# The copy of the transposed inverse in the block inverse: from VectorE to ScalarE

## The reference, cut to what matters

```
state = state * w_t + (state @ a_t) b_t + v_t k_t
y_t   = state @ r_t
```

## Time and profile before

| | |
|---|---|
| Three timed runs | 870.73, 872.73, 873.32 us; median 872.73 |
| Profiled execution | 871.72 us, its span (first to last instruction) 869.7 us |
| Granted TensorE clock | 0.997 of full speed |
| Busy share of the span | PE 99%, DVE 77%, ACT 56%, POOL 14% |

### The profile page before, as it was taken

How to read it: one execution, slowest core, us unless ns; L and a number is a source line. 1 busy time by engine, 2 the same in 40 slices (tenths; PEclk the granted TensorE clock), 3 DMA queues, 4 the chain that set the end, 5 groups by cost and what they waited for, 6 DMA issues and landing times.

```text
span 869.7 us, 19047 instructions
## 1 busy us (share of the span) xinstructions
PE 858.3 (99%) x7516; PEld 780.2 (90%) x7516; DVE 671.0 (77%) x999; ACT 486.8 (56%) x783; POOL 119.0 (14%) x136
## 2 busy tenths in 40 slices
PE   7999999999999999999999999999999999999998
PEld 7998988888888998898888888899999988899997
DVE  6996988877767776768877777787897686758876
ACT  5675465555544656745555554448824346456574
POOL 2002400000122000031000006660003500100010
PEclk9999999999999999999999999999999999999999
DMA  9543555554456542245555545576433443434461
GB/s 333 193 151 115 177 188 193 193 193 148 167 198 219 187 146 98 97 147 194 190 182 182 182 154 179 187 263 210 144 126 122 124 123 124 105 128 155 157 222 49
DMA packets 23410, 144.50 MB, mean 166 GB/s; under 512 B 2968, under 2 KB 3224, under 8 KB 9648
## 3 DMA queue, kind: packets, MB, share of 16 engines
q1 hardware_dynamic: 22032, 140.26, 47.0%
q0 software_dynamic: 1168, 3.23, 1.9%
q10 hardware_dynamic: 144, 0.06, 0.0%
HBM read 142.47 MB, written 1.06 MB: 165 GB/s over the span
## 4 chain that ended last, share of the span: by engine, by line
PE 87%; DVE 9%; ACT 1%; issue 1%; DMA 1%; SPq 0%; DVEq 0%; ACTq 0%
PE ps L615 28%; PE ps L612 14%; PE ps L602 10%; PE ps L603 10%; PE ps L604 10%; PE ps L1055 7%; DVE lo L2183 2%; DVE X L2198 1%; DMA MEM<-in_mem 1%; PE ps L758 1%; PE ps L909 1%; DVE lo L2621 1%; PE ps L759 1%; PE ps L760 1%; DVE PR L2767 1%
## 5 line engine op out<-in xcount | busy, mean ns | idle before, releaser
L615 PE MATMUL ps<-X,hi 128*128 128x512 f32 x800 | 254.7, 395 | 0.0
L2183 DVE TENSOR_TENSOR lo<-raw,hi 128x1024 fp32r<-128x1024 f32 (+1 forms) x210 | 244.1, 1204 | 10.3 <-ACT hi L1564 7.1
L612 PEld LDWEIGHTS ps<-X,lo 128*128 128x128 f32 x800 | 150.1, 188 | 32.4 <-issue 1.3
L612 PE MATMUL ps<-X,lo 128*128 128x256 f32 x800 | 165.9, 279 | 0.5 <-DVE lo L2183 0.4
L602 PE MATMUL ps<-X,hi 128*128 128x256 f32 x504 | 146.3, 290 | 0.0
L603 PE MATMUL ps<-X,hi 128*128 128x256 f32 x504 | 142.5, 283 | 0.0
L604 PE MATMUL ps<-X,lo 128*128 128x256 f32 x504 | 142.5, 283 | 0.0
L615 PEld LDWEIGHTS ps<-X,hi 128*128 128x128 f32 x800 | 125.2, 189 | 4.0
L1564 ACT ACTIVATE hi<-raw 128x1024 fp32r<-128x1024 f32 (+1 forms) x109 | 107.7, 988 | 23.7 <-DMA raw<-in_down 13.7
L615 PE MATMUL ps<-H,hi 128*128 128x512 f32 x352 | 111.5, 395 | 0.0
L1567 ACT ACTIVATE hi<-raw 128x1024 fp32r<-128x1024 f32 (+1 forms) x109 | 103.7, 951 | 0.2 <-DMA raw<-in_wide 0.2
(11 more groups left out here) (447 smaller groups left out, 1445.5 us busy)
## 6 DMA issues: line engine op xcount, KB each, us to landing
raw<-in_wide SPq DMA_DIRECT2D x106, 1024.0 KB, 4.9
raw<-in_down SPq DMA_DIRECT2D x32, 704.0 KB, 4.0
BI<-bias_table POOLq DMA_DIRECT2D x16, 128.0 KB, 4.9
raw<-in_wide SPq DMA_DIRECT2D x3, 512.0 KB, 9.1
X<-in_x SPq DMA_DIRECT2D x1, 1024.0 KB, 13.1
WG<-in_group SPq DMA_DIRECT2D x1, 768.0 KB, 17.3
out<-X SPq DMA_DIRECT2D x3, 256.0 KB, 2.4
cmask<-in_masks POOLq DMA_DIRECT2D x1, 544.0 KB, 6.7
```

The source lines that it names most:

```text
L612: nc.tensor.matmul(bank[:, 0:T], wl, x[:, 0, :], start=first, stop=False, skip_group_check=True)
L615: return nc.tensor.matmul(bank, wh, x, start=False, stop=last, skip_group_check=True)
L2183: nc.vector.tensor_tensor(lo[:, s, a:b], raw[:, s, a:b], hi[:, s, a:b].bitcast(F32), ALU.subtract).then_inc(lo_ready, 1)
```

## The change

From level 1 on, DVE only makes the masked store and raises a new semaphore of the group (`level_in` or `level_in1`). ACT waits for it, copies the second half of the bank pair to MM, and raises `taken`. ACT's handler for `level_y` did nothing before but count the use. The masked store and the copy of a group read the same pair of banks, and they still run one after the other. Level 0 stays as it was.

```diff
+        level_in, level_in1 = sem("level_in"), sem("level_in1")
...
             def level_y(g, lvl):
-                skip(A_[g])
+                if lvl == 0:
+                    skip(A_[g])
+                    return
+                fills[A_[g]] += 1
+                act.wait_ge((level_in, level_in1)[g], lvl)
+                nc.scalar.activation(MMs[g].rearrange("p h q c -> p h (q c)"), PAIR[g][:, :, T:2 * T],
+                                     ACT.Copy).then_inc(taken[A_[g]], 1)
...
                 if lvl == 0:
                     merged.then_inc(taken[b], 1)
-                    return
-                nc.vector.tensor_copy(MMs[g].rearrange("p h q c -> p h (q c)"), PAIR[g][:, :, T:2 * T]).then_inc(taken[b], 1)
+                else:
+                    merged.then_inc((level_in, level_in1)[g], 1)
```

## The result

The changed kernel takes 874.26 us (median of 22 runs) against 872.01 us (22 runs of the kernel before beside it): the ratio is 1.0025, with a 95% interval from 1.0017 to 1.0033. It is 2.2 us (1.5 to 2.9) slower, inside the 0.3% that I called "same". The forecast was a loss of 1.7 us and a time of 873.8 us, range 870.9 to 876.8.

The account below looks back on a forecast made before the run. PE, busy for 99% of the span, was taken to bound the kernel. Delays of 0.83 us at levels 3 and 4 sum to 1.66; 1.7 added to the 872.1 us mean gives 873.8 us, range 870.9 to 876.8.

Parts of the forecast that it names:

- What bounds the kernel: Whole span: PE busy for 99%; savings on DVE or ACT count only where PE waits for them, at levels 3 and 4.
- The copy's price: ACT's queue: each moved 128x512 copy from PSUM takes 0.48 us, 3.9 us for all eight.
- rival of dear copies: ACT: a copy holds the queue as long as a hi, 1.05 us; 2.8 us slower, 874.9 to 875.9; chance 15%.
- the other sum in the prediction: Levels 3 and 4: with the skill's estimated 0.73 us between second copy and hi, the loss would be 2.2 us.
- The delay of lo: DVE at levels 3 and 4: hi waits behind ACT's copies, so the first lo starts 0.83 us later at each.
- Levels 1 and 2 at nothing: Block's levels 1 and 2: lo slips some 0.6 us at level 1, but PE waits for neither engine; no cost.
- The sum: Block inverse: the delays at levels 3 and 4 add, 2 x 0.83 = 1.66 us slower.
- The rival by which PE absorbs the delay: PE at levels 3 and 4: DVE's delay goes into unseen slack; no change, 872.1 us; chance 15%.
- Where it shows: PE at level 3: stalls some 0.4 us at the product at 702.33, the rest at the transposes; one delay, not two.
- PE's waits: Block's stretch: up from 0.5 to about 2 us, at line 1196 and at the product before it.
- The rule on offloading: Skill's advice to offload a saturated DVE to Scalar; it favours the first rival, but DVE needs results from that same queue.
- offload works: DVE's first lo 0.86 us early, PE's idling before the transposes goes; at most 0.5 us plus restart, 871.5 us; chance 10%.

Follow-up runs that it names:

- the two kernels with half of the levels each: Against the kernel before, the copy moved to ACT only at levels 1 and 2 (ratio 1.0001), or only at levels 3 and 4 (ratio 1.0024).
- levels 3 and 4 alone: Against the kernel before, only levels 3 and 4 have the copy on ACT, levels 1 and 2 as before: ratio 1.0024, stretch +1.69 us.
- hi first: Against the changed kernel, ACT does the slot's hi halves ahead of the two copies at levels 1 to 4; ratio to before 0.9990, again 0.9987.

## Why the prediction was right

The time (874.26 for 873.8), the sign and the mechanism came out. Step by step:

- *What bounds the kernel.* PE, with DVE showing through, as far as the block goes, only at levels 3 and 4. Shown by the two kernels with half of the levels each.
- *The copy's price.* 0.48 us of ACT's queue was taken. The second copy starts at 695.52 and hi at 696.02: 0.50, and a copy takes 0.60 from start to end. The rival of dear copies is excluded by this row, and so is the other sum in the prediction, 2.2 us with 0.73 us ahead of hi: that it meets the timed loss is chance.
- *The delay of lo.* 0.83 us was worked out at both levels; measured 0.83 and 0.84. DVE was to idle 1.6 us for hi: 1.61.
- *Levels 1 and 2 at nothing.* Right: 0.00 us in the stretch, with the idling there in full view. The slip of lo at level 1 was 0.50 us for the 0.6 given.
- *The sum.* 1.66 us was worked out; the stretch has 1.71, the timed runs 2.2 (1.5 to 2.9). The rival by which PE absorbs the delay falls with this: PE passes both delays on whole, 0.87 and then 1.71.
- *Where it shows.* The product at 702.33 was to take some 0.4 us of the delay and the transposes the rest. At level 4 the product takes 0.56 us (1.43 less 0.87) and the transposes 0.28; at level 3 it is 0.54 and 0.33. In the changed kernel's profile the product of level 3 shows no idling that the view lists, because 0.28 us had gone before, at the pause at 696.02; with levels 3 and 4 alone that pause is not there, and the product shows 0.34 us.
- *PE's waits.* This size was wrong. They were to rise from 0.5 to about 2 us; in the same window they are 1.4 (1.0 at the transposes, 0.4 at the product), or 1.6 with the pause, though the loss came out. The idle time that a view lists is less than what a wait costs (last section).
- *The rule on offloading.* The Trainium skill, "Perfetto Trace Analysis", section "Optimizing Scalar/DVE Operations", says that moving work from a saturated DVE to Scalar may make sense. This case agrees once the order is right: the copies on ACT are then worth 0.10 and 0.13% in the two timings. What decided the sign was the work that stood behind the moved copies in ACT's queue.
- *The rival "offload works"* had the right point of decision (is hi ready when DVE has done the second masked store), and turning that point alone produced it. Its size was wrong: 0.6 to 0.7 us was given, 1.5 measured in the stretch, because PE's shown idle time was taken as the most that it could get back.

## What to carry to other kernels

Before moving an instruction to an emptier engine, look at what that engine does behind it. A wait put into an in-order queue delays everything queued there; if the engine that was to be relieved needs one of those results next, it loses more than the instruction cost. Put the moved work behind whatever is ready already, and check that what the relieved engine reads next stands ahead of the new wait.

## What was not expected

A wait on PE costs more than the idle time that the waits show. Before, the transposes at level 3 have 0.21 us of idling ahead of them, and the two heads' eight transposes with the matmuls around them run from 705.77 to 707.39:

```profile
705.77 0.28 PE L604 MATMUL ps<-X,lo 128*128 128x256 f32 x1
...
707.39 0.37 PE L602 MATMUL ps<-X,hi 128*128 128x256 f32 x1
```

With hi first nothing is late, and the same place in that kernel is:

```profile
705.83 0.28 PE L606 MATMUL ps<-X,lo 128*128 128x256 f32 x1
705.95 1.04 PE L1198 MATMUL ps<-ident,PR 128*128 128x128 f32 x8
706.74 0.36 PE L604 MATMUL ps<-X,hi 128*128 128x256 f32 x1
```

1.62 us against 0.91: 0.71 us less for 0.21 us of shown idling. Matmuls are issued before the one ahead of them has ended (a new one every 0.12 us here, each 0.28 long), and a wait takes that overlap away as well. The first transpose starts 0.48 us behind the matmul ahead of it before (705.77 to 706.25) and 0.12 with hi first (705.83 to 705.95). The other half is lost inside the line of eight: from it to the matmul behind them it is 1.14 us before and 0.79 with hi first, since the second head's rows come late too. At level 4 the same piece takes 1.67 us before and 0.91 with hi first; the two make 1.47 of the 1.5 us. This is what the rival's bound missed: it capped the gain at the idle time plus a tenth or two for restarting.
